# Two layers of a hybrid encoder: an in-projection dealt out among the other sequence's mixers, and two places that serve by turns as feed-forward input and mixer temporaries

## The reference

```python
h = rms_norm(x, norm_mix_g)
proj = h @ w_in                                   # 1024 -> 2864
aq, ak, av, bq, bk, bv, bg, ba, cq, ck, cv, co, cg = jnp.split(proj, offsets, axis=-1)
attn = axial_gqa_attention(aq, ak, av, attn_qn_g, attn_kn_g, cos, sin)   # 8 heads of 64, 2 for k, v
gla  = gla_mixer(bq, bk, bv, bg, ba, gla_gate_w2, gla_gate_b, gla_norm_g)  # 4 heads, both directions
mls  = mlstm_mixer(cq, ck, cv, co, cg, mlstm_gate_b, mlstm_norm_g)         # 4 heads, both directions
x = x + jnp.concatenate([attn, gla, mls], -1) @ w_out
u = centred_dwconv(rms_norm(x, norm_ffn_g) @ w_up, conv_w, conv_b)       # 1024 -> 5632, 3 taps
gate, val = jnp.split(u, 2, axis=-1)
x = x + (silu(gate) * val) @ w_down                                      # 2816 -> 1024
```

## Time and profile before

| what | us |
| --- | --- |
| median of three runs | 3270.96 |
| profiled execution, its own time | 3272.08 |
| its span in the trace | 3270.3 |
| PE busy (89%) | 2919.5 |
| DVE busy (58%) | 1898.7 |
| ACT busy (41%) | 1332.5 |

### The profile page before, as it was taken

How to read it: one execution, slowest core, us unless ns; L and a number is a source line. 1 busy time by engine, 2 the same in 40 slices (tenths; PEclk the granted TensorE clock), 3 DMA queues, 4 the chain that set the end, 5 groups by cost and what they waited for, 6 DMA issues and landing times. The chain is left out here.

```text
span 3270.3 us, 40480 instructions
## 1 busy us (share of the span) xinstructions
PE 2919.5 (89%) x16272; PEld 2390.7 (73%) x16272; DVE 1898.7 (58%) x3035; ACT 1332.5 (41%) x2120; POOL 0.2 (0%) x4
## 2 busy tenths in 40 slices
PE   5986469979899999998989989997989998989999
PEld 5964358968676777977866767896867677768787
DVE  4544446545556766645566677654555676555655
ACT  2243234236633554225553345323653355333332
POOL 0000000000000000000000000000000000000000
PEclk9986559989999999998999999998999999989999
DMA  4200001211121212221112211221111121132222
GB/s 134 88 33 1 1 1 67 105 45 59 46 78 59 77 59 71 88 84 39 64 53 71 71 53 65 88 101 49 53 57 65 65 71 59 65 108 92 93 95 83
DMA packets 63511, 217.19 MB, mean 66 GB/s; under 512 B 7162, under 2 KB 9210, under 8 KB 63326
## 3 DMA queue, kind: packets, MB, share of 16 engines
q1 hardware_dynamic: 63326, 214.62, 19.1%
HBM read 210.40 MB, written 4.19 MB: 66 GB/s over the span
## 5 line engine op out<-in xcount | busy, mean ns | idle before, releaser
L437 PE MATMUL ps<-hh,wlo 128*128 128x512 f32 x1696 | 695.0, 410 | 34.9 <-DVE hl L1252 32.6
L439 PE MATMUL ps<-hh,whi 128*128 128x512 f32 x1696 | 677.0, 399 | 0.0
L438 PE MATMUL ps<-hl,whi 128*128 128x512 f32 x1696 | 676.5, 399 | 0.0
L1207 DVE TENSOR_TENSOR wlo<-raw,whi 128x1024 fp32r<-128x1024 f32 x388 | 472.8, 1220 | 193.5 <-ACT whi L843 192.9
L843 ACT ACTIVATE whi<-raw 128x1024 fp32r<-128x1024 f32 x388 | 403.7, 1051 | 145.7 <-DMA raw<-d_w_units 130.1
L437 PEld LDWEIGHTS ps<-hh,wlo 128*128 128x128 f32 x1696 | 327.6, 193 | 115.8 <-DVE hl L1252 26.6
L439 PEld LDWEIGHTS ps<-hh,whi 128*128 128x128 f32 x1696 | 327.4, 193 | 72.5
L438 PEld LDWEIGHTS ps<-hl,whi 128*128 128x128 f32 x1696 | 327.6, 193 | 63.8
L437 PE MATMUL ps<-acth,wlo 128*128 128x512 f32 x704 | 301.0, 428 | 75.6 <-DVE x L1373 60.9
L1373 DVE TENSOR_TENSOR x<-x,ps 128x512 f32<-128x512 f32 x352 | 239.5, 683 | 142.2 <-PE ps L439 139.7
L438 PE MATMUL ps<-actl,whi 128*128 128x512 f32 x704 | 285.6, 406 | 0.0
(11 more groups left out here) (222 smaller groups left out, 4131.2 us busy)
## 6 DMA issues: line engine op xcount, KB each, us to landing
raw<-d_w_ffn SPq DMA_DIRECT2D x264, 512.0 KB, 3.3
raw<-d_w_units SPq DMA_DIRECT2D x124, 512.0 KB, 3.4
x<-d_x_in SPq DMA_DIRECT2D x16, 256.0 KB, 7.9
d_x_out<-x SPq DMA_DIRECT2D x16, 256.0 KB, 4.9
ropec<-d_rope SPq DMA_DIRECT2D x4, 128.0 KB, 4.1
ropes<-d_rope SPq DMA_DIRECT2D x4, 128.0 KB, 3.5
sels<-d_sel SPq DMA_DIRECT2D x1, 400.0 KB
cmask<-d_chunkmask SPq DMA_DIRECT2D x1, 256.0 KB
```

What stands on the lines that cost most here:

```text
L437: pe.matmul(out, stat[1], mov[0], start=first, stop=False)
L438: pe.matmul(out, stat[0], mov[1], start=False, stop=False)
L439: return pe.matmul(out, stat[0], mov[0], start=False, stop=last)
L1207: dve.tensor_tensor(wlo[:, SLOT[u], :, :], raw[:, SLOT[u], :].rearrange("p (k c) -> p k c", k=KT), whi[:, SLOT[u], :, :].bitcast(F32), ALU ...
```

## The change

**P1 goes into M0.** The order becomes

```diff
+REG_P = (0, 1, 1, 0)
+REG_F = (1, 0, 1, 1)
+REG_M = (0, 0, 1, 0)
+LATE_FILL = (0, NI - 1)
+PRELUDE, LEAD = 2, 5
...
+    def take(kind, n, i, width=1):
+        slot = min(range(NR - width + 1), key=lambda r: (max(used[r:r + width]), r))
+        for o in range(width):
+            used[slot + o] = len(units)
+            units.append((kind, n, i + o))
+            slots.append(slot + o)
...
-def weave(dense, mixer):
+def weave(dense, slots, mixer, over, lead=()):
...
+        if k < len(lead):
+            until = sum(lead[:k + 1])
+        else:
+            until = sum(lead) + (k + 1 - len(lead)) * (M_STEPS - sum(lead)) // (over - len(lead))
+        while mixer is not None and done < min(M_STEPS, until):
...
+        def last_reader(e):
+            kind, col = P_ITEMS[P_EVACS[e][0]]
+            if col == BV:
+                return go_psum, 2 * SB
+            if BQ <= col < BV:
+                return gx_done, 16
+            if col == CV:
+                return num_psum, 2 * MH
+            if CQ <= col < CV:
+                return stk_lo, 3 * MH
+            if col == BA:
+                return rc_ready, 1
...
+                if kind == "O" and n == 1 and i == 5:
+                    sp.wait_ge(mix_psum, 2 * SB * (n + 1))
+                    for k in range(KT):
+                        sp.dma_start(x[1][:, k, :], x_in[:, k, SEQ:T]).then_inc(x_loaded[1][k], 16)
...
-                if n < NI - 1:
+                if n not in LATE_FILL:
                     for o in range(2):
                         evacuated(n + 1, E_ALL - 4 + (o - E_ALL) % 4)
                 else:
-                    pe.wait_ge(wo_done, NI * KT)
+                    pe.wait_ge(wo_done, (n + 1) * KT)
+                    f_sums(n)
+                    yield
+                    f_spread(n)
+                    yield
...
-            in_projection(0)
-            alone(mixers(0))
+            alone(in_projection(0))
+            weave(in_projection(1), P_STEPS, mixers(0), P_STEPS - 4)
             out_projection(0)
-            for n in range(1, NI):
-                in_projection(n)
-                weave(ffn(n - 1), mixers(n))
+            weave(ffn(0), PRELUDE + F_SLOTS, mixers(1), M_OVER, (LEAD,) * PRELUDE)
+            out_projection(1)
+            for n in range(NSEQ, NI):
+                alone(in_projection(n))
+                weave(ffn(n - 1), F_SLOTS, mixers(n), M_OVER)
                 out_projection(n)
-            f_sums(NI - 1)
-            f_spread(NI - 1)
-            weave(ffn(NI - 1), None)
+            alone(ffn(NI - 1))
...
+            def fill_input(fill, n, reg, gain, k, spread_done, value, bank=7):
+                if k == 0:
+                    dve.wait_ge(spread_done, value)
+                    scaled_input(fill, n, gain, 0, bank)
+                if k + 1 < KT:
+                    scaled_input(fill, n, gain, k + 1, bank)
+                low(fill, reg, k)
...
+                        elif 11 <= i < 11 + KT:
+                            if i == 11:
+                                dve.wait_ge(wo_psum, KT * n)
+                            fill_input(FILL_F[n - 1], n - 1, REG_F[n - 1], V_FFN, i - 11, fspread, n)
```

More of the change, by code:

```diff
@@ L88, in unit_table, with stage @@
     first_unit = {}
-    def stage(kind, n, count, slot):
-        first_unit[kind, n] = len(units)
[L92 to L100, removed]
-    for n in range(1, NI):
[L102 to L105, removed]
+    used = [-NR + r for r in range(NR)]
+    def take(kind, n, i, width=1):
[4 more added lines that the diff above has]
+            slots.append(slot + o)
+    def stage(kind, n, widths):
+        first_unit[kind, n] = len(units)
+        for width in widths:
+            take(kind, n, len(units) - first_unit[kind, n], width)
+    widths = [(2, 1)[kind] for kind, _ in P_ITEMS]
+    stage("P", 0, widths)
+    stage("P", 1, widths)
+    stage("O", 0, (1,) * N_OUT)
+    for n in range(1, NI):
+        if n >= NSEQ:
+            stage("P", n, widths)
+        stage("F", n - 1, (1,) * N_FFN)
+        stage("O", n, (1,) * N_OUT)
+    stage("F", NI - 1, (1,) * N_FFN)
     return units, slots, first_unit
@@ L135, in slot_unit @@
     return base + q
-def weave(dense, mixer):
+def weave(dense, slots, mixer, over, lead=()):
     done = 0
-    for k in range(F_SLOTS):
+    for k in range(slots):
         next(dense)
-        while mixer is not None and done < M_STEPS and done < (k + 1) * M_STEPS // M_OVER:
+        if k < len(lead):
[3 more added lines that the diff above has]
+        while mixer is not None and done < min(M_STEPS, until):
             next(mixer)
             done += 1
+    while mixer is not None and done < M_STEPS:
+        next(mixer)
+        done += 1
     for gen in (dense, mixer):
@@ L148, in weave, with alone @@
             assert next(gen, None) is None
[L151 to L154, removed]
+def alone(gen):
+    for _ in gen:
+        pass
 def build(nc, x_in, w_units, w_ffn, vecs, w2p, qkg, convp, rope, gmask, chunkmask, lmask, sel,
@@ L226, in build @@
[L226 to L234, removed]
@@ L254, in build @@
+        H, MIXED, ATT, GLA, LSTM = zip(*[places(r) for r in range(2)])
         ps = ctx.enter_context(nc.psum_tensor("ps", [P, 8, 512], F32))
@@ L1169, in mixers @@
                     yield
-            p_squares(0)
+            def mixers(n):
+                yield from (gla(n) if n == 0 else attention(n))
+                yield from (mlstm(n) if n == 0 else gla(n))
+                yield from (attention(n) if n == 0 else mlstm(n))
+                yield from mix(n)
+            for k in range(KT):
+                p_square(0, k)
             p_roots(0)
@@ L1319, in out_projection @@
+                    for _ in range(4):
+                        yield
             def out_projection(n):
@@ L1699, in mixers @@
                     yield
-            p_add_squares(0)
+            def mixers(n):
+                yield from (gla(n) if n == 0 else attention(n))
+                yield from (mlstm(n) if n == 0 else gla(n))
+                yield from (attention(n) if n == 0 else mlstm(n))
+                yield from mix(n)
+            for k in range(KT):
+                p_add_square(0, k)
             p_diagonals(0)
-            dve.wait_ge(pspread, 1)
             for k in range(KT):
-                scaled_input(FILL_P[0], 0, V_MIX, k)
+                fill_input(FILL_P[0], 0, REG_P[0], V_MIX, k, pspread, 1)
                 if k == 3:
```

630 lines of the change are left out of this document (369 added, 261 removed).

## The result

The changed kernel takes 3157.54 us (median of four runs, 3153.34 to 3160.11), the kernel before, in the same comparison, 3271.89; the ratio is 0.965 (0.9633 to 0.9667). That is 114 us faster; 128 were forecast. The profiled execution has a span of 3157.0 us against 3270.3.

| | before | after | moved | forecast |
| --- | --- | --- | --- | --- |
| start | 41.6 | 40.3 | -1.3 | -1.9 |
| P0 | 132.0 | 133.5 | +1.5 | 0 |
| M0 and P1 (W) | 457.0 | 375.4 | -81.7 | -105 |
| O0 | 46.7 | 45.0 | -1.6 | 0 |
| F0 with M1 | 596.5 | 602.2 | +5.7 | +13 |

What follows compares the result with a forecast made beforehand. M0 was taken as the one long stretch bound by a chain between PE, ACT and DVE, half its span at 1.2 GHz. 3272.1 - 105 - 1.9 + 13 - 28 - 5.8 = 3144 us, range 3105 to 3195.

Steps and rivals of the forecast that it cites:

- W: Weave of P1 with M0: 352 us in place of 457, from 288 PE work, 39 unfilled waits, 25 other engines.
- PE's own work: In the weave: 131.7 us for P1 and 156 for the mixers, together 288 us.
- The rotations, priced at 9: In the weave: P1's four rotations fall where DVE must answer PE's scores; half of 17 us is 9.
- the 13 us for the rest of P1's DVE and ACT work: In the weave: of 98.6 us of P1's DVE and ACT work, 13 us delay the mixers' chain.
- The low clock costs nothing extra where PE waits anyway: In the weave: no further term taken for PE's low clock level.
- The rival of the low clock: PE stays at its low level through the whole weave: W = 535, 3327 us, slower; chance 0.04.
- F0, +13 forecast: F0 with M1: a new 40.8 us head loses 30.3, the old start's 16.8 lost go; net +13 us.
- F1 and F2, -28: Starts of F1 and F2: inputs filled earlier, in P2 and P3, save 14 us each, -28 us.
- F3, -5.8: F3's head: the longest unused weight slot lets sums start 2.2 us after O3's last matmul, -5.8 us.
- nearly every wait is filled: Rival for the weave: P1's work fills nearly every wait, W = 300, 3092 us; chance 0.07.
- P1's work on DVE and ACT lands on the chain whole: Rival for the weave: all that work delays the mixers' chain, W = 426, 3218 us; chance 0.13.
- nothing overlaps: Rival for the weave: PSUM copies wait for the first sequence's readers, W = 457, 3249 us; chance 0.03.

Runs made afterwards that it cites:

- e11: The changed kernel with e5's deal and the second in-projection's four rotations moved into the out-projection O0, whose squares stand behind them: 3128.91 us (ratio 0.9565).
- e5: The changed kernel with more of P1's pieces beside GLA's chunk steps (27 and 28 instead of 20 each), fewer in mLSTM and attention: 3147.28 us (ratio 0.9625).
- e1: The changed kernel with the weave undone, M0 alone and P1 alone behind it: 3233.87 us (one run).
- e2: The changed kernel with 28 of P1's pieces (instead of 11) ahead of GLA's first key transposes and fewer beside its chunks: 3188.97 us (ratio 0.9748).
- e10: The changed kernel without the ten mixer steps of M1 ahead of F0: 3147.17 us (ratio 0.9615).
- e9: The changed kernel with the inputs of F1 and F2 filled late again, in the feed-forward's first eight pieces: 3191.00 us (one run).
- e8: The kernel before with one edit alone, weight units taking the slot used longest ago: 3269.03 us (one run).
- e12: The changed kernel with e11's edits and no mixer steps of M1 ahead of F0: 3124.51 us (ratio 0.9548).

## Why the prediction was right, and which terms were off

The bound was read rightly: the time came from M0's stretch, and no other stage moved by more than 15.3 us. All the directions held; F0's size was half. The total came out some 13 us above the forecast: W did 23 us worse and F0 7 better. W would have been forecast another 16 us too low had PE's own work not been taken too high; that this error stood against that of the clock is luck.

- **W, 352 forecast, 375.4 measured.** Its waits were forecast at 39 + 25 = 64 us and measured at 65.0, but the parts differ, so the equal sum is luck too: the rows' wait nearly went (8.6 forecast, 2.5 measured), those before mLSTM's scores grew (2.2 forecast, where four times 0.5 is 2.0; 12.3 measured), and that for the first keys was right (11.8, 12.5). The rotations, priced at 9, cost 9.5 us of waits (e11 against e5); the 13 us for the rest of P1's DVE and ACT work and the 2.6 for table loads are not told apart by any run. PE's own work was taken as 288 and is 271.7 at full clock: P1 alone is 125.9 (e1), not 131.7, and the mixers in the weave 146 instead of 156. The 156 was a misreading of the clock in the trace of before: it took off the low level of F0's first 31.7 us alone, but PE worked 49.1 us at that level in the whole stage and 14.0 in F3. Half of each taken off gives 514.1 - 368.5 = 146. The sum over the 11 stretches at the lower level in F0 with M1:

```profile
sum 58.04, PE 49.13 PEld 38.46 DVE 25.64 ACT 18.75 POOL 0.00; mean PE 4.47 PEld 3.50 DVE 2.33 ACT 1.70 POOL 0.00
```

- **The step that failed** is "The low clock costs nothing extra where PE waits anyway, and no more term is taken for it". It cost 38.7 us by the half taken above, 36.4 by the straight line of the last section. The rival of the low clock was thus partly there: not through the whole weave but in 95.6 of its 375.4 us, and in 77.4 of these PE did not wait. The Trainium skill (TensorE: Matmul & The Clock Gate, HAM oscillation) tells of falls behind pauses of PE; the stretch from 192.33 agrees, since it begins in the wait of 12.5 us that started at 188.31. That a pause is not needed is shown by e2's fall at 240.88, 27 us behind PE's last wait.
- **F0, +13 forecast, +5.7 measured.** The head took 37.2 us, not 40.8, and the stage behind it 565.1. The forecast implies 569.2 there: the 564.8 of before behind the start of 31.7 us, with 14.9 of work that had stood in that start, and without 10.5 for ten steps. Why it took 4 us less is not shown. PE's rows of the head: sums, the first and the last of the four groups of transposes, the spread, the first dense matmul:

```profile
596.49 1.02 PE L505 MATMUL ps<-ones,psqsum 128*128 128x1 f32 x8 [2.27 <-DVE psqsum L1376]
599.74 1.97 PE L701 MATMUL ps<-ident,qd 128*128 128x128 f32 x8 [2.23 <-DVE kd L1582]
...
615.57 1.94 PE L701 MATMUL ps<-ident,qd 128*128 128x128 f32 x8 [2.47 <-DVE qs L1589]
...
618.15 1.45 PE L511 MATMUL ps<-pdiag,ones 128*128 128x512 f32 x2
...
631.37 0.47 PE L498 MATMUL ps<-hh,wlo 128*128 128x512 f32 x1 [2.58 <-DVE hl L1403]
```

  The order is the one forecast: the groups come 5.3 us apart, each held up by the copies of the one before, and the dense work stands behind all of it. That e10 is better than this and than before shows the price to be the steps' place.
- **F1 and F2, -28.** Measured -28.3, and 33 come back when it is undone (e9).
- **F3, -5.8.** Measured -6.6. 5.8 are the slot (e8); the rest is that the sums ran in 1.02 us, where they had taken 1.86 at the lower level.
- **Nothing for P0 and O0.** P0 got 1.5 us longer and O0 1.6 shorter, since the ten small matmuls moved; DVE's 79.5 us in P0 stayed hidden.
- **Start, -1.9.** Measured -1.3.

The rivals that nearly every wait is filled (W = 300) and that P1's work on DVE and ACT lands on the chain whole (W = 426) are excluded by W itself; that nothing overlaps, by e1. What of the 65 us of waits could still be filled is open: e2 filled more of them and lost by the clock, and a deal that does both was not found within these runs.

## What to carry to other kernels

When dense work is dealt out among a chain's steps, look at what clock PE is granted in each stretch, not only at where it waits: a stretch of tiny matmuls can stand at the lower level without a pause of PE, and 7 or 8 pieces more beside each set of 16 steps shortened the weave by 14 us. Side work of a vector engine (here rotations) is best put into a stage where the matrix engine waits for it in nothing: the same four rotations cost 13 to 18 us of the weave (e12 and e11 against e5), some 10 of them waits, and left the out-projection as long as it was. Steps put ahead of a stage to cover its head can cost more than the head: these ten made it 37 us instead of 9, and leaving them out shortened the stage by 11.

## What the runs showed of the hardware that I had not expected

PE's granted clock fell 27 us behind PE's last wait (e2, at 240.88), and it stood at 0.5 for 58 us in which PE was busy without a pause (e2, from 275.01), while it ran GLA's matmuls of 64 and 128 columns with 114 of P1's 128x256 between them; with 245 between the same ones (e5) it stood at 1.0. PE's work in W, counted at full clock (busy time less half of low work), came to 267 to 272 us in eleven kernels whose busy time there ran from 286 to 341 us, so work at the lower level takes close to twice as long (a straight line through the eleven gives 0.47 in place of the half). From one of P1's 128x256 matmuls to the next it is 213 ns at the lower level and 114 at the higher (medians in e2's W), 1.87 times. And with equal instructions low work in W still differed from run to run (28.1 and 40.7 us in e11 and e12).
